# Retention scores as one product over all 128 rows, with q copied into a zero-padded buffer

## What is computed

```python
# q, k (B, S, 4 heads, 64) rotated; v (B, S, 4, 128); chunks of C = 128 tokens, N = 4 of them
qf = q.reshape(B, N, C, H, dk);  kf = (k * dk ** -0.5).reshape(B, N, C, H, dk)
scores = jnp.einsum('bnihd,bnjhd->bnhij', qf, kf) * decay[None, None]
inner = jnp.einsum('bnhij,bnjhe->bnihe', scores, vf)
...                                    # kv and the state r_prev carried from chunk to chunk
cross = jnp.einsum('bnihd,hi,bnhde->bnihe', qf, xi, r_prev)
out = (inner + cross).reshape(B, S, H, dv)
out = out * lax.rsqrt(jnp.mean(out * out, axis=-1, keepdims=True) + EPS)
```

## Time and profile before

| | |
|---|---|
| median of 3 runs | 304.5 us (302.53 to 304.65) |
| span of the profiled execution, first to last instruction | 300.2 us |
| mean granted TensorE clock over the span | 0.989 |
| TensorE busy | 288.5 us, 96% of the span |
| VectorE busy | 204.2 us, 68% |
| ScalarE busy | 146.3 us, 49% |
| GpSimd busy | 71.6 us, 24% |

### The profile page before, as it was taken

How to read it: one execution, slowest core, us unless ns; L and a number is a source line. 1 busy time by engine, 2 the same in 40 slices (tenths; PEclk the granted TensorE clock), 3 DMA queues, 4 the chain that set the end, 5 groups by cost and what they waited for, 6 DMA issues and landing times.

```text
span 300.2 us, 4549 instructions
## 1 busy us (share of the span) xinstructions
PE 288.5 (96%) x1551; PEld 246.4 (82%) x1551; DVE 204.2 (68%) x434; ACT 146.3 (49%) x328; POOL 71.6 (24%) x133
## 2 busy tenths in 40 slices
PE   7898999999999999997999999999999999999992
PEld 6898888888878888886888888798888888888891
DVE  1884788999999999559984862638646525843441
ACT  4876764532735525562566444465442671441231
POOL 0066742363310029991200002010010020000111
PEclk9799999999999999999999999999999999999997
DMA  6852650053044054040304220030210315411113
GB/s 234 300 226 72 209 145 1 0 157 125 14 141 127 2 151 130 1 140 3 102 37 142 70 70 0 4 140 4 75 64 2 90 52 178 170 35 39 71 76 134
DMA packets 14230, 28.01 MB, mean 93 GB/s; under 512 B 1016, under 2 KB 2560, under 8 KB 14208
## 3 DMA queue, kind: packets, MB, share of 16 engines
q1 hardware_dynamic: 13632, 26.95, 27.7%
q10 hardware_dynamic: 576, 0.79, 0.7%
HBM read 25.63 MB, written 2.10 MB: 92 GB/s over the span
## 4 chain that ended last, share of the span: by engine, by line
PE 74%; DVE 12%; issue 3%; ACT 2%; POOL 0%; DVEq 0%; ACTq 0%; POOLq 0%
PE bank L389 18%; PE bank L391 18%; PE bank L390 18%; PE bank L434 6%; DVE keys L940 4%; DVE top L938 3%; PE bank L448 3%; DVE w_lo L857 3%; PE bank L462 2%; PE bank L475 2%; PE bank L463 2%; DVE k_stack L902 1%; PE bank L496 1%; PE bank L509 1%; PE bank L410 1%
## 5 line engine op out<-in xcount | busy, mean ns | idle before, releaser
L389 PE MATMUL bank<-w_hi,xT_hi 128*128 128x512 f32 (+2 forms) x328 | 127.4, 388 | 2.7 <-DVE w_lo L857 1.9
L391 PE MATMUL bank<-w_hi,xT_lo 128*128 128x512 f32 (+2 forms) x328 | 124.3, 379 | 0.0
L390 PE MATMUL bank<-w_lo,xT_hi 128*128 128x512 f32 (+2 forms) x328 | 124.1, 378 | 0.0
L389 PEld LDWEIGHTS bank<-w_hi,xT_hi 128*128 128x128 f32 x328 | 62.0, 189 | 14.1 <-issue 3.1
L391 PEld LDWEIGHTS bank<-w_hi,xT_lo 128*128 128x128 f32 x328 | 61.9, 189 | 11.4
L390 PEld LDWEIGHTS bank<-w_lo,xT_hi 128*128 128x128 f32 x328 | 62.1, 189 | 9.9
L857 DVE TENSOR_TENSOR w_lo<-w_raw,w_hi 128x1024 fp32r<-128x1024 f32 (+1 forms) x40 | 47.4, 1204 | 14.3 <-ACT w_hi L559 14.1
L559 ACT ACTIVATE w_hi<-w_raw 128x1024 fp32r<-128x1024 f32 (+1 forms) x40 | 40.3, 1023 | 5.1 <-PE bank L391 3.2
L667 ACT ACTIVATE work<-work,small 128x128 f32<-128x128 f32 (+3 forms) x32 | 17.8, 556 | 34.7 <-DVE small L963 34.7
L806 POOL TENSOR_TENSOR th<-zt,tab 128x64 f32<-128x64 f32 (+2 forms) x32 | 16.6, 519 | 59.1 <-ACT zt L600 56.1
L762 POOL TENSOR_SCALAR small<-small 128x1 f32<-128x1 f32 (+1 forms) x8 | 2.7, 343 | 106.7 <-ACT junk L688 92.6
(11 more groups left out here) (103 smaller groups left out, 342.3 us busy)
## 6 DMA issues: line engine op xcount, KB each, us to landing
w_raw<-in_w_in SPq DMA_DIRECT2D x28, 512.0 KB, 3.6
w_raw<-in_w_out SPq DMA_DIRECT2D x8, 512.0 KB, 3.7
retT<-in_x SPq DMA_DIRECT2D x8, 256.0 KB, 4.0
x_h<-in_x SPq DMA_DIRECT2D x3, 512.0 KB, 5.7
w_raw<-in_w_in SPq DMA_DIRECT2D x4, 324.0 KB, 4.7
out<-x_h SPq DMA_DIRECT2D x4, 320.0 KB, 2.5
out<-x_h ACTq DMA_DIRECT2D x4, 192.0 KB, 2.7
tab<-in_table SPq DMA_DIRECT2D x1, 691.0 KB, 7.1
```

What stands on the lines that cost most here:

```text
L389: pe.matmul(o, xh, hi[:, kk, c0:c0 + w], start=first, stop=False)
L390: pe.matmul(o, xh, lo[:, kk, c0:c0 + w], start=False, stop=False)
L391: mm = pe.matmul(o, xl, hi[:, kk, c0:c0 + w], start=False, stop=last)
```

## The change

The four 64-row products of a chunk become two over all 128 rows, one for each pair of heads. The stationary operand is the whole `krT[:, p, chunk]`, with both heads' keys in it. The moving operand is 256 columns of a new buffer `q_pad`: in its columns for the lower head the upper 64 partitions are zero, and in those for the upper head the lower 64. So the result has the same two heads side by side. GpSimd clears `q_pad` once and copies q into its two non-zero parts for every chunk (`pad_q`, two copies of 64 partitions x 256 elements). There is one buffer, so the copy for chunk n + 1 waits for the scores of chunk n. All scores of a chunk now stand ahead of the attention's transposes.

```diff
+        q_pad = sb("q_pad", [P, 2, 2, P])
...
-            def ret_scores(n, hh):
-
-                r = slice(64 * hh, 64 * hh + 64)
-                if hh:
-                    pe.wait_ge(st_mm, 2 * n + 1)
-                else:
-                    pe.wait_ge(t_evac, 4 * MT)
-                    if n >= 1:
-                        pe.wait_ge(y_ret_psum, n)
-                for h in (hh, hh + 2):
-                    mm = pe.matmul(mid_ps[:, h * P:(h + 1) * P], krT[r, h // 2, n * P:(n + 1) * P],
-                                   qrT[r, h // 2, n * P:(n + 1) * P], start=True, stop=True)
+            def ret_scores(n):
+
+                pe.wait_ge(t_evac, 4 * MT)
+                pe.wait_ge(q_padded, 2 * (n + 1))
+                if n >= 1:
+                    pe.wait_ge(y_ret_psum, n)
+                for p in range(2):
+                    mm = pe.matmul(mid_ps[:, 2 * p * P:2 * (p + 1) * P], krT[:, p, n * P:(n + 1) * P],
+                                   q_pad[:, p, :, :], start=True, stop=True)
                 mm.then_inc(st_mm, 1)
...
                 if retention and (g - RET0) % 2 == 0:
-                    ret_scores((g - RET0) // 2, 0)
+                    ret_scores((g - RET0) // 2)
                 if 0 <= g - ATT0 - 1 < STEPS:
                     transpose_probs(g - ATT0 - 1)
-                if retention and (g - RET0) % 2 == 0:
-                    ret_scores((g - RET0) // 2, 1)
...
+            pool.memset(q_pad[:, :, :, :], 0.0).then_inc(q_pad_zeroed, 1)
             pool.memset(minus_half, -0.5).then_inc(minus_half_done, 1)
...
+            def pad_q(n):
+
+                if n:
+                    pool.wait_ge(st_mm, n)
+                else:
+                    pool.wait_ge(q_pad_zeroed, 1)
+                    pool.wait_ge(qx_done, MT)
+                for hh in range(2):
+                    if hh:
+                        pool.wait_ge(q_padded, 2 * n + 1)
+                    r = slice(64 * hh, 64 * hh + 64)
+                    pool.tensor_copy(q_pad[r, :, hh, :], qrT[r, :, n * P:(n + 1) * P]).then_inc(q_padded, 1)
+                pool.wait_ge(q_padded, 2 * n + 2)
+
+            pad_q(0)
             pool.wait_ge(t_done, 4 * MT)
             pool.memset(zt[:, :, :], 0.0).then_inc(state_zeroed, 1)
 
             for n in range(MT):
 
+                if n < MT - 1:
+                    pad_q(n + 1)
                 pool.wait_ge(ret_sq, RH * (n + 1))
...
-                dve.wait_ge(st_mm, 2 * n + 2)
+                dve.wait_ge(st_mm, n + 1)
```

More of the change, by code:

```diff
@@ L257, in hymba_layer @@
         tanh_done, rgate_done, agate_psum = sems("tanh_done rgate_done agate_psum")
+        q_pad_zeroed, q_padded = sems("q_pad_zeroed q_padded")
         state_zeroed, st_mm, st_evac, kv_mm, state_step = sems("state_zeroed st_mm st_evac kv_mm state_step")
```

## The result

Nine runs each: the changed kernel 300.48 us (299.55 to 302.09), the kernel before 302.7 us (301.92 to 304.65), six more runs of before having brought its median down from 304.5. The ratio is 0.992, with a 95% interval from 0.989 to 0.994; a second session gave 0.990 (0.987 to 0.993). So the kernel is 0.8 to 1.0% faster, clear of noise: 2.5 and 3.1 us by the ratios, 2.2 and 3.1 us between the medians. Forecast were 301.5 us and a gain of 3.0 us, with "within 1%" as the likeliest class. Four executions of all sessions, at 325.1 to 581.7 us and all of kernels with the 64-row products, are left out of every ratio.

What follows compares the result with a forecast made beforehand. TensorE's own work was taken to bound the retention's slots: removing 6.4 us and adding 3.4 us brings the span from 300.2 to 297.2 us and the median from 304.5 to 301.5 us, range 300.2 to 303.3 us.

Steps and rivals of the forecast that it cites:

- within 1%: Whole kernel: the outcome class of a time within about 1% of the time before, given chance 0.54.
- What bounds it: Retention's slots: TensorE is busy 75.00 of 75.00 us from 150 to 225 us, so its own work sets the time.
- What is removed: TensorE, retention scores: L475's products and the surplus at their neighbours go, 1.61 us a chunk, 6.44 us for four.
- What is added: TensorE, retention scores: two 128-row, 256-column products at L493's pace, 0.86 us a chunk, 3.44 us for four.
- The upper end: New score products on TensorE: at most 1.29 us a chunk, with a border of 0.2 us kept on either side.
- What is late next: Chunk 2's chains over VectorE and GpSimd: L1041 keeps 0.57 us and L1013 0.72 us ahead of TensorE; nothing lost.
- Rival 5: Measured level: a median of a few runs comes out 0.6 us or more below 301.5 us; chance 0.10.
- the full gain: Whole kernel: all 3.0 us saved on TensorE arrive, 301.5 us, with 300.9 to 302.1 for spread; chance 0.66.
- VectorE held up: Chunk 2's chain: GpSimd's copies delay VectorE, TensorE loses up to 0.9 us once, 301.6 to 302.4 us; chance 0.13.
- the slower case: GpSimd and VectorE lock: copies hold VectorE up to 3.44 us a chunk in three chunks, 310.1 us; chance 0.03.
- A border's cost kept: New score products on TensorE: they cost 1.29 us a chunk, so the time is 303.2 us; chance 0.05.
- Records only: TensorE around the scores: the surplus is an effect of the records only, time stays at 304.5 us; chance 0.03.

Runs made afterwards that it cites:

- the run in one row: Kernel before, with all four 64-row score products together ahead of the transposes, without the wait, all reading the lower 64 partitions: ratio 0.996 (0.993 to 0.999).

## Why the prediction was right, and where it was wrong

In short: the mechanism and nearly the size were right, 3.0 us forecast and 2.74 in the chain. The step that failed is the one from this sum to the chances: "About 1% either way is what a measurement of this kernel can tell from no change". The runs tell no change to 0.25 to 0.3%, so a gain of 0.8% stands clear of it, while the forecast had "within 1%", which reads like no change, as its likeliest class. Two terms were off besides, the cost of L474 and the level.

**What bounds it: right.** TensorE's saving in the retention, 2.74 us in the chain, arrives in the time: 0.8 and 1.0% in two sessions.

**What is removed: right.** 1.61 us a chunk, of which 0.75 are surplus. That it sits at the borders between 64-row and 128-row products is shown by the run in one row (0.34 us for a way in and back, and none for each further 64-row product) and by the padded products, which have none in either place. That there are two products for four saves next to nothing: eight passes of 128 columns at the pace of L496 are 0.88 us, the padded four of 256 take 0.86 to 0.92. A part that I did not name is in it: grouping the halves showed that the wait for the first group and the change of the half can cost as much as a border.

**What is added: the first term that was mis-sized.** "I take 0.86, since L493 is the same product in the same surroundings." It measured 0.92. The surroundings are not the same: L493 comes behind 512- or 384-column products, L474 behind the 64-column ones of L436, and only behind these does it cost 0.06 us more. Four chunks make 0.24 us. The upper end that the prediction gave for this term was also summed wrong: 0.86 with 0.2 us on either side is 1.26 and not 1.29.

**GpSimd: right.** 0.4 us a copy, all of it hidden, up to six times as many.

**What is late next: half right.** L1041 of chunk 2 was ahead by 0.48 us (0.57 forecast), L1013 of the same chunk by 0.72, as forecast. But "the place to look at is chunk 2" failed as a claim about the nearest limit: the last L912 of chunk 0 was done 0.69 us before its product; what stands ahead of the product became 0.50 us shorter (0.64, 0.58 and 0.64 us became 0.92 and 0.44), and the border that lengthened the product itself, 0.19 us, is gone too. So TensorE reaches it just as VectorE ends, and waits; the first L464 takes 0.27 us in place of 0.18. That is 0.09 us of the four chunks' gain, which the prediction put at nothing. Its row was in the trace; I followed the waits of the retention's own chain and not every wait in the slot that became shorter.

**The level and the chances: wrong.** 3.0 us were forecast, 2.74 found in the chain and 2.5 and 3.1 in the two ratios, but 301.5 us is 1.0 us above the measured median. I took it from 304.5, a median of three runs of which two were high; nine gave 302.7. In every execution since, the time is the span plus 1.8 us (302.09 and 300.3 in the changed kernel), so the 300.2 us of the span belonged to a run of 302.0, and "4.3 us above the span" joined two different executions. Rival 5 had warned that a median of a few runs can come out 0.6 us or more below 301.5. The measured 300.48 us falls in that rival's part of the range and not in the 300.9 to 302.1 of the full gain; that it lies inside the range at all owes to the room left for that rival and not to the sum. And the step that failed, named above: the intervals are 0.25 to 0.3% wide on either side, and the prediction names no row for its 1%. A gain of 0.8 to 1.0% is well outside the intervals, so I was wrong to let the likeliest class read like no change.

**Rivals.** VectorE held up, and the slower case: refuted, by six times the copies. A border's cost kept: refuted, 0.92 and not 1.29. Records only: refuted by the runs. More than the sum: the gain itself was not more; only the level was lower, as told above.

What stays open is why TensorE's clock falls behind the idle time near 138 us in some executions and not in others. In the profiles here it did so in two of nine with 1.7 us of idle time (the changed kernel's first one, and at 0.89 over 134 to 150 us the one without scores), and in none of the three with 1.2 us. Three are too few to tell.

## What to carry to other kernels

Before a product of half the rows is called half the work, add up the chain of waits in a slot with it and in a slot without it: here the neighbours paid 0.33 us of the 1.61, and zero padding to full height, with the same columns, took 0.69 us of it away for the price of a copy on an idle engine. Where a slot becomes shorter by some time, go through every wait in it and behind it for those that are met by less than that time, also of work that has nothing to do with the change. Take the level from many runs, and look in the profile for stretches where the clock or the start differs before two spans are compared.

## What was not expected of the hardware

- The first 256-column fp32 product behind a row of 64-column products takes 0.06 us more than behind 128-column transposes (0.49 against 0.43 for its two passes).
- GpSimd's copies and VectorE's instruction with two SBUF inputs: VectorE lost 0.08 us, GpSimd 0.9 us for a pair. With GpSimd's two-input L808, of 512 elements, VectorE lost up to 1.0 us (1.68 against 0.69). The Trainium skill says on its page "SBUF — State Buffer", under "Who interferes with whom", that the shared pair of ports is an exclusive lock and that the order of issue decides who waits. The rows with L808 agree: L928 starts at 134.19 while L808 runs (133.71 to 135.32) and ends 0.55 us behind it. The copies agree in part: L873 starts at 171.06, 0.23 us ahead of the first copy's end, and loses 0.09 us, not 0.23; the second copy takes 1.28 us and ends 0.25 us behind L873.
- The granted clock fell to half for about 3 us behind 1.67 us of idle time in one execution, which cost 1.5 us, and stayed full behind 1.73 us in another of the same kernel.
